# The state products of the sample tokens in one rounded pass over 128 rows, and the prompt's gated states on 128 rows

## The chip, the cores and the metric

The kernel runs on one core of one Trainium2 chip. The metric is the device time of one launch in microseconds (us); lower is better. The kernel before took 2338.71 us, the median of three runs (2337.27 to 2346.19).

The engines are called here as the profile calls them: PE is TensorE's matmul side and PEld its weight loads, DVE is VectorE, ACT ScalarE, POOL GpSimd, SP SyncE.

## The reference

Two layers of a decoder trunk run on 512 prompt tokens and on 8 sequences of 4 new tokens ("the sample", 32 tokens in all). Per layer: a feed-forward block, a token mixer, a second feed-forward block. The mixer has four gated heads (GLA: keys of 64, values of 128) and four retention heads (keys and values of 128). Both keep a state of keys by values:

```
S_new = decay * S + einsum('bhsk,bhsv->bhkv', k * exp(b_last - b), v)
o     = o_inter(q, S) + einsum('bhts,bhsv->bhtv', A, v)
```

The prompt starts from zero states and goes through them in chunks; each of the 8 sample sequences has its own given states (state_gla, state_ret), which are read for the outputs, updated with 4 tokens each, and returned.

## The kernel before, in words

**Numbers.** All is float32. The weight products, nearly all of the work, are done with operands split in two rounded parts of type fp32r, a high and a low one: three products (high by high, low by high, high by low) replace one float32 product. All are issued on L500. The weights come by DMA into `raw`, ACT copies the high part into `w_hi` (L937), POOL subtracts to get `w_lo` (L445), and PE works through units of 8 key tiles with them. The small products of the mixer are plain float32; the profile lists two records for each of these.

**Mixer stage.** After the input projection (29 tiles of output, with the gates' and scores' steps between them) the prompt runs through four chunks of 128 tokens, c = 0 to 3, and the sample is a fifth step, S. For each chunk there are four PE steps, kept in the order written in TAIL_STEPS (for DVE and ACT in TAIL_HALF_STEPS):

- turn c: 14 transposes of values and keys to token-major form in PSUM; ACT copies them to `v_tok` and `k_tok` (L1085, L1087), DVE multiplies the retention keys with their decay (L1411).
- scores c: retention scores (L711), which DVE masks, and the chunk's state deltas (L717 retention, L722 gated), which DVE adds to the decayed states (L1446, L1453). `s_gla` holds the two heads of a pair one above the other: head p has partitions p*64 to p*64+63.
- out c: for each gated head a 128-row product of scores and values (L740) and, from chunk 1 on, a 64-row product of queries and state (L742); for each retention head two 128-row products (L747, L749).
- back c: outputs, scaled to unit mean square by ACT and DVE (squares L1092, sum L1463, root L1098 and L1101, product L1473), are transposed back (L763) and gated by DVE (L1485).

**Sample.** turn S gives `v_tok_s` and `k_tok_s`, 32 tokens on 32 partitions. Out S runs one product of scores and values per head (L776) and one per head and sequence with that sequence's state (L784, queries of the other sequences being zero), 64 rows for a gated and 128 for a retention head. POOL prepares these masked queries (mask_queries, L453 to L462), after `o_ready` of chunk 2. ACT starts the loads of the given states as soon as the last input tile is read (L1181, L1184).

**The sample's state deltas.** For each of the 8 heads, in UPDATE_ORDER (retention first), DVE spreads the head's values over 8 blocks of 128 columns, zero where a token is not of that block's sequence (mask_values, L1500), and PE multiplies the keys with two halves of 512 columns (sample_delta, L808): contraction over 32 tokens, float32. DVE adds the result to the state (L1511, L1517), ACT stores it. Delta 0 stands behind out S and is followed by two filler products (L519, keep_clock_up); deltas 1 to 7 stand behind the first seven of the eight units of the output projection. PE is in order, so a delta's time there is added to the projection's.

**Start.** ACT makes `half_gain`, half of the gains of all norms, once at the start (L1134). DVE converts the masks (L1550) before it waits for the first norm.

Of the kernel before, what the change touches and what calls it, by code (L numbers as in the profile page):

```python
# [28 lines left out]
P = 128  # L29
# [32 lines left out]
def trunk_kernel(nc, x_prompt, x_sample, state_gla, state_ret, norm_g, w1_gu, w1_down, w2_gu, w2_down,  # L62
# [64 lines left out]
    S = NCH  # L127

# [21 lines left out]
    with ExitStack() as ctx:  # L150
# [9 lines left out]
        def overlay(*tensors):  # L160
# [19 lines left out]
        half_gain = sb("half_gain", [P, DEPTH * NN * KD])  # L180
        chunk_decay = sb("chunk_decay", [P, QT, NCH + NS])
        rms = sb("rms", [P, 2, HA])
# [8 lines left out]
        ret_state, gla_state, v_tok_s, k_tok_s = overlay(  # L191
            ("ret_state", [P, HR, NS, DV], F32), ("gla_state", [P, QT, NS, DV], F32),
            ("v_tok_s", [TS, HA, P], F32), ("k_tok_s", [TS, HR * P + QT * P], F32))
# [20 lines left out]
        v_tok, k_tok, a_ret, s_gla, s_ret, o_tok = overlay(  # L214
# [3 lines left out]
            ("s_gla", [P, 2, QT, DV], F32), ("s_ret", [P, 2, HR, DV], F32),  # L218
            ("o_tok", [P, HA, P], F32))
# [15 lines left out]
        def v_by_batch(i):  # L235

            return v_tok[0:TS, (i + 1) % 2].rearrange("p h v -> p (h v)")[:, 0:NS * DV].rearrange("p (b v) -> p b v", b=NS)
# [24 lines left out]
        def post_gain(l, q, k):  # L262

            table = vecs if q == 1 else half_gain
            return table[:, bass.ds(l * (NN * KD) + ((2 * q + 1) * KD + k), 1)]
# [10 lines left out]
        x_turned = sem("x_turned")  # L276
        w_a2_loaded, a_loaded = sem("w_a2_loaded"), sem("a_loaded")
# [33 lines left out]
        o_turned, o_gated = sig("o_turned", NSTEP), sig("o_gated", NSTEP)  # L311
        v_masked, s_delta, s_updated = sig("v_masked", HA), sig("s_delta", HA), sig("s_updated", HA)
# [65 lines left out]
        STATE_DMAS = (2 + QT + HR) * 16  # L378
# [56 lines left out]
        def _(pool):  # L435
# [11 lines left out]

            def mask_queries(l):
# [39 lines left out]
        def _(pe):  # L488
# [192 lines left out]
            def turn(l, c_):  # L681
# [6 lines left out]
                elif c_ == 1:  # L688
                    wait(pe, o_normed, l, 0)
                elif c_ == 2:  # L690
                    wait(pe, in_read, l, NIN - 1)
                    wait(pe, o_gated, l, 0)
                else:
                    wait(pe, o_normed, l, c_ - 2)
                    wait(pe, o_gated, l, c_ - 2)
                for h in range(HA):
                    pe.transpose(ps[0:n, b0 + h // 4, h % 4 * P:(h % 4 + 1) * P], v_t[:, h, t0:t0 + n], ident)  # L697
                for h in range(HR):
                    pe.transpose(ps[0:n, b0 + 2, h * P:(h + 1) * P], k_r[:, h, t0:t0 + n], ident)
                for q in range(QT):  # L700
                    mm = pe.transpose(ps[0:n, b0 + 3, q * P:(q + 1) * P], k_dec[:, q, t0:t0 + n], ident)
# [24 lines left out]
            def out(l, c_):  # L726
# [9 lines left out]
                for h in range(HG):  # L736
# [30 lines left out]
            def out_sample(l, part):  # L767
# [4 lines left out]
                for h in range(part * HA // 2, (part + 1) * HA // 2):  # L772
# [3 lines left out]
                    pe.matmul(o, a_gla_s[:, p, q, :] if h < HG else a_ret_s[:, h - HG, :], v_tok_s[:, h, :], start=True,  # L776
                              stop=False)
# [16 lines left out]
            def sample_delta(l, i):  # L794

                h = UPDATE_ORDER[i]
                wait(pe, v_masked, l, i)
                if i >= 2:
# [3 lines left out]
                if h < HG:  # L802
                    p = h % 2
                    keys, r0, r1 = k_tok_s[:, HR * P + h * DKG:HR * P + (h + 1) * DKG], p * DKG, (p + 1) * DKG
                else:
# [100 lines left out]
        def _(act):  # L906
# [168 lines left out]
            def act_step(l, kind, c_):  # L1075
                n, b0 = TS if c_ == S else CH, BANK0[c_]
                if kind == "turn":
# [5 lines left out]
                    vt, kt = (v_tok_s, k_tok_s) if c_ == S else (v_tok[:, c_ % 2], k_tok)  # L1083
                    for i in range(2):
                        act.activation(vt[0:n, 4 * i:4 * i + 4, :],  # L1085
                                       ps[0:n, b0 + i, :].rearrange("p (h v) -> p h v", v=DV), ACT.Copy)
                    act.activation(kt[0:n, HR * P:(HR + QT) * P], ps[0:n, b0 + 3, 0:QT * P], ACT.Copy)\  # L1087
                        .then_inc(v_tok_ready.sem, 1)
# [15 lines left out]
                if kind == "root" and c_ == NCH - 1:  # L1104

                    wait(act, state_ready, l, c_)
                    act.dma_start(gla_p[l, 0].rearrange("(q p) k v -> (p k) q v", p=2), s_gla[:, c_ % 2, :, :])\
                        .then_inc(states_stored, 16)
# [25 lines left out]
            act.activation(half_gain[:, :], vecs[:, 0:DEPTH * NN * KD], ACT.Copy, scale=0.5).then_inc(vec_ready, 1)  # L1134
# [74 lines left out]
        def _(dve):  # L1209
# [192 lines left out]
            def turn_keys(l, c_):  # L1402
# [4 lines left out]
                if c_ == S:  # L1407
                    wait(dve, v_tok_ready, l, c_)
                n, b0 = TS if c_ == S else CH, BANK0[c_]
                kt, decay = (k_tok_s, c("k_decay_s", TS)) if c_ == S else (k_tok, c("k_decay"))  # L1410
                o = dve.tensor_tensor(kt[0:n, 0:HR * P].rearrange("p (h k) -> p h k", h=HR),  # L1411
                                      ps[0:n, b0 + 2, :].rearrange("p (h k) -> p h k", h=HR),
                                      decay.rearrange("p (h k) -> p h k", k=1).broadcast_to([n, HR, P]), ALU.mult)
                o.then_inc(k_tok_ready.sem, 1)
# [18 lines left out]
            def update_states(l, c_):  # L1433
# [7 lines left out]
                for q in range(QT):  # L1441
                    delta = ps[:, b0 + 3, (QT + q) * DV:(QT + q + 1) * DV]
                    if c_ == 0:
                        dve.tensor_copy(s_gla[:, new, q, :], delta)
                    else:
                        dve.scalar_tensor_tensor(out=s_gla[:, new, q, :], in0=s_gla[:, old, q, :],  # L1446
                                                 scalar=chunk_decay[:, q, c_:c_ + 1], in1=delta, op0=ALU.mult, op1=ALU.add)
# [47 lines left out]
            def mask_values(l, i):  # L1495

                h = UPDATE_ORDER[i]
                if i >= 2:
                    wait(dve, s_delta, l, i - 2)
                dve.tensor_tensor(v_by_batch(i), v_tok_s[:, h:h + 1, :].broadcast_to([TS, NS, DV]),  # L1500
                                  c("batch_mask", TS).rearrange("p (b x) -> p b x", x=1).broadcast_to([TS, NS, DV]),
# [19 lines left out]
            def dve_step(l, kind, c_):  # L1521
                if kind == "turn":
                    turn_keys(l, c_)
                elif kind == "scores":
                    decay_scores(l, c_)
                elif kind == "state":
# [21 lines left out]
            add_x_squares(0, 0)  # L1548
            dve.wait_ge(masks_loaded, 16)
            dve.tensor_copy(msk[:, :], mask_rows[:, :])  # L1550
            for l in range(DEPTH):
# [153 lines left out]
```

## Time and profile before

| | |
|---|---|
| median of three runs | 2338.71 us |
| profiled execution, its time | 2346.03 us |
| profiled execution, its span | 2344.2 us |
| PE busy | 2285.5 us (97%) |
| DVE busy | 820.4 us (35%) |
| ACT busy | 799.7 us (34%) |
| POOL busy | 943.7 us (40%) |
| DMA | 197.58 MB, mean 84 GB/s |

The profile is one execution, and its time is 7.3 us above the median of the runs. "Busy" of PE counts overlapped, modelled ends of matmuls, so the distance between starts tells more than durations do. PEclk is the clock granted to TensorE: 1.00 is 2.4 GHz and 0.50 is 1.2 GHz. The idle time in brackets at a row is that of the engine just before it, with what ended it.

### The profile page before, as it was taken

To read this page: it belongs to the slowest core of one execution; us is meant where nothing else is said; L and a number is where in the kernel's file an instruction comes from. 1 tells how busy PE (TensorE), PEld (TensorE's weight loads), DVE (VectorE), ACT (ScalarE), POOL (GpSimd) and SP (SyncE) were. 2 spreads that over 40 slices of the span, in tenths; PEclk is the share of its full clock that TensorE was granted. 3 is DMA by queue.
4 is the path that set the end of the run, shared out by engine and by line. 5 is a ranking of instruction groups with operands and counts; after the bars stand their busy time and mean duration, and the time that the engine had idled before them with its cause. 6 is when DMAs were issued, how large, how long until landed. Compare 5 with 4: busy or idle time off the path is not lost.

```text
span 2344.2 us, 43364 instructions
## 1 busy us (share of the span) xinstructions
PE 2285.5 (97%) x17703; PEld 2219.5 (95%) x17703; DVE 820.4 (35%) x1115; ACT 799.7 (34%) x1380; POOL 943.7 (40%) x770
## 2 busy tenths in 40 slices
PE   8999999999989999999999999999999999999998
PEld 8999999999968899999999999999998779999998
DVE  4222200687334522220052222017864454222102
ACT  4333333442312433233343333334323234333333
POOL 3444444344113344444534444443541124444442
PEclk9999999999989999999999999999999999999999
DMA  5323223222303223322322332332223132323222
GB/s 171 86 84 89 74 86 96 78 82 64 99 26 100 79 83 89 89 71 87 109 76 82 89 89 70 92 109 55 82 73 81 52 99 81 88 82 89 74 88 75
DMA packets 382556, 197.58 MB, mean 84 GB/s; under 512 B 8836, under 2 KB 381368, under 8 KB 382328
## 3 DMA queue, kind: packets, MB, share of 16 engines
q1 hardware_dynamic: 353200, 180.64, 26.8%
q10 hardware_dynamic: 29256, 15.49, 2.4%
q8 instruction: 77, 1.26, 0.2%
q14 instruction: 23, 0.19, 0.0%
HBM read 186.80 MB, written 9.31 MB: 84 GB/s over the span
## 4 chain that ended last, share of the span: by engine, by line
PE 93%; DVE 4%; ACT 1%; issue 1%; ACTq 0%; DMA 0%; DVEq 0%
PE ps L500 84%; PE ps L784 2%; PE ps L808 1%; PE ps L658 1%; DVE x L1275 1%; DVE xs_lo L1213 1%; DVE y L1269 0%; DVE y_out L1269 0%; PE ps L740 0%; PE ps L742 0%; PE ps L633 0%; PE ps L697 0%; DVE q_lvl L1360 0%; PE ps L763 0%; PE ps L747 0%
## 5 line engine op out<-in xcount | busy, mean ns | idle before, releaser
L445 POOL TENSOR_TENSOR w_lo<-raw,w_hi 128x512 fp32r<-128x512 f32 (+1 forms) x728 | 915.7, 1263 | 1281.5 <-ACT w_hi L937 1281.4
L500 PE MATMUL ps<-xs_hi,w_hi 128*128 128x256 f32 (+1 forms) x3712 | 789.6, 290 | 16.5 <-DVE xs_lo L1213 13.1
L500 PE MATMUL ps<-xs_lo,w_hi 128*128 128x256 f32 (+1 forms) x3712 | 786.4, 289 | 0.0
L500 PE MATMUL ps<-xs_hi,w_lo 128*128 128x256 f32 (+1 forms) x3712 | 784.2, 288 | 0.0
L937 ACT ACTIVATE w_hi<-raw 128x512 fp32r<-128x512 f32 (+1 forms) x728 | 420.8, 586 | 964.5 <-PE ps L500 964.0
L500 PEld LDWEIGHTS ps<-xs_hi,w_hi 128*128 128x128 f32 x3712 | 598.5, 188 | 25.4 <-DVE xs_lo L1213 15.2
L500 PEld LDWEIGHTS ps<-xs_hi,w_lo 128*128 128x128 f32 x3712 | 600.6, 188 | 0.0
L500 PEld LDWEIGHTS ps<-xs_lo,w_hi 128*128 128x128 f32 x3712 | 599.9, 188 | 0.2
L1234 DVE TENSOR_TENSOR tmp<-ps,rstd_pre 128x544 f32<-128x544 f32 x88 | 63.8, 725 | 642.4 <-PE ps L500 627.4
L500 PE MATMUL ps<-h_lo,w_hi 128*128 128x256 f32 x1272 | 267.4, 289 | 0.0
L500 PE MATMUL ps<-h_hi,w_lo 128*128 128x256 f32 x1272 | 266.6, 288 | 0.0
L500 PE MATMUL ps<-h_hi,w_hi 128*128 128x256 f32 x1272 | 266.5, 288 | 0.0
L500 PEld LDWEIGHTS ps<-h_hi,w_lo 128*128 128x128 f32 x1272 | 205.1, 188 | 0.0
L500 PEld LDWEIGHTS ps<-h_lo,w_hi 128*128 128x128 f32 x1272 | 204.8, 188 | 0.0
L500 PEld LDWEIGHTS ps<-h_hi,w_hi 128*128 128x128 f32 x1272 | 204.5, 188 | 0.0
L1254 DVE TENSOR_TENSOR acc<-acc,sq 128x544 f32<-128x544 f32 x30 | 21.8, 726 | 357.7 <-ACT sq L1020 357.7
L1240 DVE TENSOR_TENSOR tmp<-tmp 128x544 f32<-128x544 f32 x88 | 96.2, 1093 | 11.8 <-ACT tmp L981 4.1
L983 ACT ACTIVATE h_hi<-tmp 128x544 f32 (+1 forms) x88 | 57.9, 658 | 112.6 <-DVE tmp L1240 112.6
L1243 DVE TENSOR_TENSOR h_lo<-tmp,h_hi 128x544 f32 x88 | 64.0, 727 | 83.8 <-ACT h_hi L983 83.8
L1020 ACT ACTIVATE sq<-ps 128x544 f32<-128x544 f32 (+2 forms) x54 | 31.0, 575 | 148.1 <-PE ps L500 148.1
L1236 DVE TENSOR_TENSOR tmp<-ps,rstd_pre 128x544 f32<-128x544 f32 x88 | 62.9, 715 | 0.0
L981 ACT ACTIVATE tmp<-tmp 128x544 f32<-128x544 f32 x88 | 58.1, 660 | 11.1 <-DVE tmp L1234 0.9
(181 smaller groups left out, 1761.3 us busy)
## 6 DMA issues: line engine op xcount, KB each, us to landing
raw<-in_w_gu_dram SPq DMA_DIRECT2D x176, 512.0 KB, 3.8
raw<-in_w_in_dram SPq DMA_DIRECT2D x56, 512.0 KB, 3.8
raw<-in_w_down_dram SPq DMA_DIRECT2D x64, 384.0 KB, 3.4
raw<-in_w_down_dram SPq DMA_DIRECT2D x64, 320.0 KB, 3.1
raw<-in_w_out_dram SPq DMA_DIRECT2D x16, 512.0 KB, 3.9
ret_state<-in_state_ret_dram ACTq DMA_DIRECT2D x8, 512.0 KB, 6.1
out_dram<-ret_state ACTq DMA_DIRECT2D x8, 512.0 KB, 3.2
x_tok<-in_x_prompt_dram SPq DMA_DIRECT2D x4, 512.0 KB, 6.3
```

What stands on the lines that cost most here:

```text
L445: pool.tensor_tensor(lo, raw[:, u, k0:k0 + n, :], hi.bitcast(F32), ALU.subtract)\
L500: mm = pe.matmul(bank_part(bank, a), w, v[:, kx, TOK[a]], start=(start and n == 0), stop=(stop and n == 2))
L658: mm = pe.matmul(ps[:, 4 + 2 * (n % 2) + c_ // 2, at:at + CH].rearrange("p (a t) -> p a t", a=2), k_lvl[:, hh, c_ * CH:(c_ + 1) * CH], q_l ...
L784: mm = pe.matmul(o, queries, state, start=False, stop=(b == NS - 1))
L937: act.activation(hi, raw[:, u, k0:k0 + n, :], ACT.Copy).then_inc(hi_split, 1)
L981: act.activation(tmp[:, 0, :], tmp[:, 0, :], ACT.Silu).then_inc(gate_silu.sem, 1)
L983: act.activation(h_hi[:, bass.ds(i * 2 + par, 1), :], tmp[:, 0:1, :], ACT.Copy).then_inc(hh_ready.sem, 1)
L1020: act.activation(sq[:, m % 2, cols], pair(m % 2)[:, cols], ACT.Square).then_inc(y_sq.sem, 1)
L1234: dve.tensor_tensor(tmp[:, 0, :], pair(2 * par), rstd_pre[:, :], ALU.mult)\
L1236: dve.tensor_tensor(tmp[:, 1, :], pair(2 * par + 1), rstd_pre[:, :], ALU.mult)\
L1240: dve.tensor_tensor(tmp[:, 0, :], tmp[:, 0, :], tmp[:, 1, :], ALU.mult).then_inc(h_prod.sem, 1)
L1243: dve.tensor_tensor(h_lo[:, tile, :], tmp[:, 0:1, :], h_hi[:, tile, :].bitcast(F32), ALU.subtract)\
```

## The change

The sample's state deltas get a rounded (fp32r) product over 128 rows. The 32 tokens are put four times on the partitions, so that rows 0 to 31, 32 to 63, 64 to 95 and 96 to 127 hold the same tokens. The values' high part stands on the first two quarters and their low part on the last two; the keys' high part stands on quarters 0 and 2 and their low part on 1 and 3. One product of such operands sums all four combinations of high and low. For that POOL writes the tokens four times before the transposes (spread_sample), turn S transposes all 128 columns, ACT rounds and DVE subtracts. Second, `s_gla` is laid out by head: each head has a plane of 128 partitions, of which the other head's 64 are zero, so that out c uses the full `q_dec` with 128 rows. Third, `half_gain` goes: the gains of the outer norms are halved in place.

The diff, cut to its core:

```diff
@@ pool
+            def spread_sample(l):
+                wait(pool, in_read, l, NIN - 1)
+                for n, src, dst in ((HA, v_t, v_spread), (HR, k_r, k_spread[:, 0:HR, :]), (QT, k_dec, k_spread[:, HR:HR + QT, :])):
+                    o = pool.tensor_copy(dst.rearrange("p h (o t) -> p h o t", o=QUADS),
+                                         src[:, :, TP:T]....broadcast_to([P, n, QUADS, TS]))
+                o.then_inc(rows_spread.sem, 1)
...
+                        spread_sample(l)
                         mask_queries(l)
@@ pe, turn
+                if c_ == S:
+                    wait(pe, rows_spread, l, 0)
-                    pe.transpose(ps[0:n, b0 + h // 4, h % 4 * P:(h % 4 + 1) * P], v_t[:, h, t0:t0 + n], ident)
+                    pe.transpose(ps[:, b0 + h // 4, h % 4 * P:(h % 4 + 1) * P],
+                                 v_t[:, h, t0:t0 + n] if c_ < S else v_spread[:, h, :], ident)
...
@@ pe, out
-                        pe.matmul(o, q_dec[p * DKG:(p + 1) * DKG, q, t0:t0 + CH],
-                                  s_gla[p * DKG:(p + 1) * DKG, (c_ - 1) % 2, q, :], start=False, stop=True)
+                        pe.matmul(o, q_dec[:, q, t0:t0 + CH], s_gla[:, (c_ - 1) % 2, p, q, :], start=False, stop=True)
@@ pe, sample_delta
+                if i == 0:
+                    wait(pe, k_low, l, 0)
...
-                    keys, r0, r1 = k_tok_s[:, (h - HG) * P:(h - HG + 1) * P], 0, P
+                tile = HR + h // 2 if h < HG else h - HG
+                keys = k_split[:, tile * P:(tile + 1) * P]
                 for a in range(2):
-                    mm = pe.matmul(ps[r0:r1, 4 + 2 * (i % 2) + a, :], keys,
+                    mm = pe.matmul(ps[:, 4 + 2 * (i % 2) + a, :], keys,
                                    v_by_batch(i)[:, a * NS // 2:(a + 1) * NS // 2, :], start=True, stop=True)
@@ act, turn S
+                        for i in range(2):
+                            o = act.activation(v_split[:, 4 * i:4 * i + 4, :],
+                                               ps[:, b0 + i, :].rearrange("p (h v) -> p h v", v=DV), ACT.Copy)
+                    o.then_inc(v_tok_ready.sem, 1)
+                    if c_ == S:
+                        act.activation(k_split[:, KR:KR + KG], ps[:, b0 + 3, 0:KG], ACT.Copy)
+                        wait(act, k_decayed, l, 0)
+                        act.activation(k_split[:, 0:KR], tmp[:, 0, 0:KR], ACT.Copy).then_inc(k_high.sem, 1)
@@ act, store of the prompt's gated state: two DMAs of 64 partitions in place of one of 128
@@ act, start
-            act.activation(half_gain[:, :], vecs[:, 0:DEPTH * NN * KD], ACT.Copy, scale=0.5).then_inc(vec_ready, 1)
+            for l in range(DEPTH):
+                for n in (1, 5):
+                    g = vecs[:, (l * NN + n) * KD:(l * NN + n + 1) * KD]
+                    act.activation(g, g, ACT.Copy, scale=0.5).then_inc(vec_ready, 1)
@@ dve, turn_keys: the decay multiplies 128 rows into tmp, ahead of the wait for v_tok_ready; then
+                low = slice(P // 2, P)
+                dve.tensor_tensor(v_split[low, :, :], ps[low, b0:b0 + 2, :].rearrange("p a (h v) -> p (a h) v", v=DV),
+                                  v_split[low, :, :].bitcast(F32), ALU.subtract).then_inc(k_tok_ready.sem, 1)
+            def low_keys(l):
+                wait(dve, k_high, l, 0)
+                for at in (TS, 3 * TS):
+                    low = slice(at, at + TS)
+                    dve.tensor_tensor(k_split[low, 0:KR], tmp[low, 0, 0:KR], k_split[low, 0:KR].bitcast(F32), ALU.subtract)
+                    o = dve.tensor_tensor(k_split[low, KR:KR + KG], ps[low, BANK0[S] + 3, 0:KG],
+                                          k_split[low, KR:KR + KG].bitcast(F32), ALU.subtract)
+                o.then_inc(k_low.sem, 1)
@@ dve, update_states: for each pair q, one operation of 64 partitions per head p in place of one of 128
@@ dve, mask_values
-                dve.tensor_tensor(v_by_batch(i), v_tok_s[:, h:h + 1, :].broadcast_to([TS, NS, DV]),
+                dve.tensor_tensor(v_by_batch(i), v_split[:, h:h + 1, :].bitcast(F32).broadcast_to([P, NS, DV]),
@@ dve, start, behind add_x_squares(0, 0)
+            dve.memset(s_gla.rearrange("p n h q v -> p (n h q v)"), 0.0).then_inc(s_zeroed, 1)
+            dve.wait_ge(s_zeroed, 1)
...
+            dve.wait_ge(tables_loaded, 16)
+            for i in range(1, QUADS):
+                for name in ("k_decay_s", "batch_mask"):
+                    o = dve.tensor_copy(cst[i * TS:(i + 1) * TS, cc[name][0]:cc[name][1]], c(name, TS))
```

low_keys runs on DVE right behind decay_scores of S. `v_by_batch` now uses all 128 partitions of the two buffers that lie over `v_tok`, and is of type fp32r. The first two ACT copies of turn S (32 rows, for out S) stay.

## Rows read from the trace of the kernel before

**Rows 1.** The page: busy time of each engine, and the chain that ended last.
```profile
PE 2285.5 (97%) x17703; PEld 2219.5 (95%) x17703; DVE 820.4 (35%) x1115; ACT 799.7 (34%) x1380; POOL 943.7 (40%) x770
...
PE ps L500 84%; PE ps L784 2%; PE ps L808 1%; PE ps L658 1%; DVE x L1275 1%; DVE xs_lo L1213 1%; DVE y L1269 0%; DVE y_out L1269 0%; PE ps L740 0%; PE ps L742 0%; PE ps L633 0%; PE ps L697 0%; DVE q_lvl L1360 0%; PE ps L763 0%; PE ps L747 0%
```

**Rows 2.** Windows, out S, layers 0, 1: stretch, length; PE, PEld, DVE, ACT, POOL; PEclk.
```profile
668.07:694.59 26.52, 26.52 (x153) 19.67 (x153) 4.92 (x6) 0.80 (x3) 0.00 (x0) 0.68 0.06 15
1826.78:1845.32 18.54, 18.54 (x153) 15.08 (x153) 4.92 (x6) 0.80 (x3) 0.00 (x0) 1.00 0.08 23
```

**Rows 3.** Timeline of PE, output projection, layer 0: start, duration, instructions.
```profile
708.92 0.41 PE L500 MATMUL ps<-o_hi,w_lo 128*128 128x256 f32 x2
709.27 1.98 PE L808 MATMUL ps<-v_tok,k_tok_s 32*128 32x512 f32 x4
711.18 0.52 PE L500 MATMUL ps<-o_hi,w_hi 128*128 128x256 f32 x2
711.53 0.41 PE L500 MATMUL ps<-o_lo,w_hi 128*128 128x256 f32 x2
711.78 0.41 PE L500 MATMUL ps<-o_hi,w_lo 128*128 128x256 f32 x2
...
733.63 1.93 PE L808 MATMUL ps<-v_tok,k_tok_s 32*64 32x512 f32 x4
```

**Rows 4.** Timeline of PE, layer 1: out 2, scores 3, back 2.
```profile
1806.83 0.39 PE L740 MATMUL ps<-v_tok,a_gla 128*128 128x128 f32 x2
...
1810.39 0.39 PE L749 MATMUL ps<-s_ret,q_r 128*128 128x128 f32 x2
...
1811.95 1.06 PE L711 MATMUL ps<-q_r,k_r 128*128 128x128 f32 x8
...
1816.49 1.07 PE L763 MATMUL ps<-cst,o_tok 128*128 128x128 f32 x8 [1.37 <-issue]
```

**Rows 5.** Timelines of ACT and PE behind out 1, layers 0 and 1.
```profile
636.77 1.09 ACT L1092 ACTIVATE sq<-ps 128x512 f32<-128x512 f32 x2 [6.93 <-issue]
...
639.85 2.04 PE L711 MATMUL ps<-q_r,k_r 128*128 128x128 f32 x8 [2.73 <-DVE k_tok L1411]
...
644.00 1.09 PE L763 MATMUL ps<-cst,o_tok 128*128 128x128 f32 x8
...
1793.23 3.73 ACTq L1184 DMA_DIRECT2D gla_state<-in_state_gla_dram  x2
...
1800.16 1.13 PE L711 MATMUL ps<-q_r,k_r 128*128 128x128 f32 x8 [1.59 <-DVE k_tok L1411]
...
1802.71 1.09 PE L763 MATMUL ps<-cst,o_tok 128*128 128x128 f32 x8
```

**Rows 6.** Timelines of PE and ACT, layer 0: turn S to the start of out S.
```profile
660.43 1.03 PE L697 MATMUL ps<-cst,v_t 128*32 128x128 f32 x8 [1.15 <-DVE v_t L1485]
...
662.16 1.06 ACT L1085 ACTIVATE v_tok_s<-ps 32x512 f32<-32x512 f32 x2 [5.80 <-PE ps L701]
...
667.17 0.44 PE L711 MATMUL ps<-q_r,k_r 128*32 128x32 f32 x8
668.07 0.37 PE L776 MATMUL ps<-v_tok_s,a_gla_s 32*32 32x128 f32 x2 [0.46 <-DVE a_ret_s L1421]
```

**Rows 7.** Timeline of PE, layer 1: delta 0 and back S, behind out S.
```profile
1845.32 1.98 PE L808 MATMUL ps<-v_tok,k_tok_s 32*128 32x512 f32 x4
...
1849.76 0.65 PE L763 MATMUL ps<-cst,o_tok 32*128 32x32 f32 x8 [1.40 <-DVE o_tok L1473]
```

**Rows 8.** Timelines of POOL and DVE, output projection; last row: DVE at the start.
```profile
719.32 3.58 POOL L445 TENSOR_TENSOR w_lo<-raw,w_hi 128x512 fp32r<-128x512 f32 x2 [4.54 <-ACT w_hi L937]
...
735.60 2.15 DVE L1511 SCALAR_TENSOR_TENSOR gla_state<-gla_state,chunk_decay,ps 64x128 f32<-64x128 f32 x8 [0.48 <-PE ps L808]
737.67 1.51 DVE L1500 TENSOR_TENSOR v_tok<-v_tok_s,cst 32x1024 f32<-32x1024 f32 x1
...
40.40 0.72 DVE L1234 TENSOR_TENSOR tmp<-ps,rstd_pre 128x544 f32<-128x544 f32 x1 [4.03 <-ACT rstd_pre L921]
```

More of the change, by code:

```diff
@@ L127, in trunk_kernel @@
     S = NCH
+    QUADS = P // TS
+    KR, KG = HR * P, QT * P
     IN_ORDER = (1, 2, 3, 0) + tuple(range(4, NIN))
@@ L212, in trunk_kernel @@
             ("w_a2_sb", [2 * GR, QT * P], F32))
-        v_tok, k_tok, a_ret, s_gla, s_ret, o_tok = overlay(
+        v_tok, k_tok, a_ret, s_ret, o_tok, rms, v_ret_s = overlay(
             ("v_tok", [P, 2, HA, P], F32),
@@ L217, in trunk_kernel @@
             ("a_ret", [P, HR, CH], F32),
[L218 to L219 removed]
+            ("s_ret", [P, 2, HR, DV], F32),
+            ("o_tok", [P, HA, P], F32), ("rms", [P, 2, HA], F32), ("v_ret_s", [TS, HR, P], F32))
+        v_rows, = overlay(("v_rows", [P, 2, HA, P], F32R))
         _, y_out, o_lo, o_hi = overlay(("ahead_of_v_t", [P, 7 * QT * T + QT * HALF], F32), ("y_out", [P, KD, T], F32),
@@ L262, in post_gain @@
         def post_gain(l, q, k):
-            table = vecs if q == 1 else half_gain
-            return table[:, bass.ds(l * (NN * KD) + ((2 * q + 1) * KD + k), 1)]
+            return vecs[:, bass.ds(l * (NN * KD) + ((2 * q + 1) * KD + k), 1)]
+        tables_spread = sem("tables_spread")
         tables_loaded, masks_loaded, x_loaded = sem("tables_loaded"), sem("masks_loaded"), [sem(f"x_loaded{i}") for i in range(X_PARTS)]
@@ L311, in trunk_kernel @@
         o_turned, o_gated = sig("o_turned", NSTEP), sig("o_gated", NSTEP)
+        rows_spread = sig("rows_spread", 1)
+        k_decayed, k_high, k_low = sig("k_decayed", 1), sig("k_high", 1), sig("k_low", 1)
         v_masked, s_delta, s_updated = sig("v_masked", HA), sig("s_delta", HA), sig("s_updated", HA)
@@ L775, in out_sample @@
                     o = ps[0:TS, BANK0[S] + 2 * a, i * DV:(i + 1) * DV]
-                    pe.matmul(o, a_gla_s[:, p, q, :] if h < HG else a_ret_s[:, h - HG, :], v_tok_s[:, h, :], start=True,
-                              stop=False)
+                    pe.matmul(o, a_gla_s[:, p, q, :] if h < HG else a_ret_s[:, h - HG, :],
+                              v_gla_s[:, h, :] if h < HG else v_ret_s[:, h - HG, :], start=True, stop=False)
                     for b in range(NS):
@@ L1082, in act_step @@
                         wait(act, o_ready, l, c_ - 2)
-                    vt, kt = (v_tok_s, k_tok_s) if c_ == S else (v_tok[:, c_ % 2], k_tok)
                     for i in range(2):
[L1085 to L1088, printed above, removed]
+                        vt = (v_gla_s, v_ret_s)[i] if c_ == S else v_tok[:, c_ % 2, 4 * i:4 * i + 4, :]
+                        o = act.activation(vt[0:n, :, :],
+                                           ps[0:n, b0 + i, :].rearrange("p (h v) -> p h v", v=DV), ACT.Copy)
+                    if c_ < S:
+                        o = act.activation(k_tok[:, KR:KR + KG], ps[:, b0 + 3, 0:KG], ACT.Copy)
+                    else:
+                        for i in range(2):
[6 more added lines that the diff above has]
+                        act.activation(k_split[:, 0:KR], tmp[:, 0, 0:KR], ACT.Copy).then_inc(k_high.sem, 1)
                 elif kind == "squares":
@@ L1106, in act_step @@
                     wait(act, state_ready, l, c_)
-                    act.dma_start(gla_p[l, 0].rearrange("(q p) k v -> (p k) q v", p=2), s_gla[:, c_ % 2, :, :])\
-                        .then_inc(states_stored, 16)
+                    for p in range(2):
+                        act.dma_start(gla_p[l, 0].rearrange("(q p) k v -> p k q v", p=2)[p],
+                                      s_gla[p * DKG:(p + 1) * DKG, c_ % 2, p, :, :]).then_inc(states_stored, 16)
                     act.dma_start(ret_p[l, 0].rearrange("h k v -> k h v"), s_ret[:, c_ % 2, :, :])\
@@ L1406, in turn_keys @@
                     wait(dve, state_delta, l, c_ - 1)
[L1407 to L1414, printed above, removed]
+                b0 = BANK0[c_]
+                kt, decay = (tmp[:, 0, 0:KR], c("k_decay_s")) if c_ == S else (k_tok[:, 0:KR], c("k_decay"))
+                o = dve.tensor_tensor(kt.rearrange("p (h k) -> p h k", h=HR),
+                                      ps[:, b0 + 2, :].rearrange("p (h k) -> p h k", h=HR),
+                                      decay.rearrange("p (h k) -> p h k", k=1).broadcast_to([P, HR, P]), ALU.mult)
+                if c_ < S:
+                    o.then_inc(k_tok_ready.sem, 1)
+                    return
+                o.then_inc(k_decayed.sem, 1)
+                wait(dve, v_tok_ready, l, c_)
+                low = slice(P // 2, P)
[9 more added lines that the diff above has]
+                o.then_inc(k_low.sem, 1)
             def decay_scores(l, c_):
@@ L1442, in update_states @@
                     delta = ps[:, b0 + 3, (QT + q) * DV:(QT + q + 1) * DV]
[L1443 to L1447, printed above, removed]
+                    for p in range(2):
+                        rows = slice(p * DKG, (p + 1) * DKG)
+                        if c_ == 0:
+                            dve.tensor_copy(s_gla[rows, new, p, q, :], delta[rows])
+                        else:
+                            dve.scalar_tensor_tensor(out=s_gla[rows, new, p, q, :], in0=s_gla[rows, old, p, q, :],
+                                                     scalar=chunk_decay[rows, q, c_:c_ + 1], in1=delta[rows],
+                                                     op0=ALU.mult, op1=ALU.add)
                 for h in range(HR):
@@ L1525, in dve_step @@
                     decay_scores(l, c_)
+                    if c_ == S:
+                        low_keys(l)
                 elif kind == "state":
```

31 lines of the change are left out of this document (18 added, 13 removed).

## The prediction, made before the kernel after was run

> **What bounds the kernel now.** I read the page first, then the windows over out S, then PE's timeline stretch by stretch, and the other engines only where PE stood idle. On the page PE is busy for 97% of the span and the chain of waits lies on it; DVE, ACT and POOL are busy for 34 to 40% [rows 1]. So a microsecond taken from PE is a microsecond of the kernel wherever PE runs without a gap, and nothing where PE then waits for a chain that hasn't become shorter. The reader is to see two things in the rows. One is distances between starts: durations overlap. The other is the brackets: 2.73, 1.59, 1.37, 0.46 and 1.40 us are the gaps in the mixer's tail [rows 4 to 7].
>
> The profiled execution took 2346.03 us (span 2344.2 and 1.8 around it), 7.3 above the median of 2338.71. The windows show where: out S ran the same 153 matmuls in 26.52 us in layer 0 and 18.54 in layer 1, at a mean granted clock of 0.68 and of 1.00 [rows 2]. 2346.03 - 7.98 = 2338.05, the time of the two faster runs. So two of the three timed runs most likely lack this stretch at 1.2 GHz. I make the sum as a difference, check it against the profile, and take it from the median.
>
> **The state deltas, L808.** In the projection a delta takes from 709.27 to 711.18, 1.91 us in four records; a gated head's lasts 1.93 in place of 1.98, so 1.86 [rows 3]. It also slows its neighbours. A pair of L500 records (256 and 288 columns) goes in 0.25 us, 711.53 to 711.78; the pair ahead of the delta takes 0.35 to its start (708.92 to 709.27) and the pair behind it 0.35 (711.18 to 711.53) [rows 3]. I count these 0.2 as the cost of going from 128 rows to 32 and back, and they go. Together 2.11 and 2.06 us. In its place come two fp32r products of 512 columns over 128 rows. L500 is just such a product: 544 columns in 0.25, so 512 in 0.235 and two in 0.47 us. Gain 1.64 for a retention head and 1.59 for a gated one. Bounds: above, 1.91 if the products were free; below, 0.2 if they stayed as dear as the float32 ones and only the neighbours gained. I take 1.6, since L500's row is the same kind. Deltas 1 to 7 lie in the projection: 3 x 1.64 + 4 x 1.59 = 11.3 per layer, **22.6 us** for two.
>
> Delta 0 gives nothing. It stands behind out S, where PE waits 1.40 us for back S [rows 7]: ACT's squares, DVE's sum, the root and the norm product are all released by out S's end, not by the delta. 4.44 us after that end back S starts, before and after; the gap becomes about 2.9 us.
>
> What must keep up is the projection's period: (733.63 - 709.27) / 3 = 8.12 us now, about 6.5 then [rows 3]. POOL needs 3.58 in one (two rests), DVE 0.7 for the squares' sum, 2.15 for a gated state and 1.51 for a mask, 4.4 together [rows 8]. A mask on 128 rows in place of 32 has the same 1024 columns; I cost it the same, and at double it is 5.9, still below 6.5. Nothing new ends last.
>
> **Out c, L742.** Out 2 takes 1806.83 to 1811.95 = 5.12 us. The 18 records of its start, in which 128-row and 64-row products alternate, take 3.56 (0.198 each); the remaining 14, all on 128 rows, 1.56 (0.111 each) [rows 4]. On 128 rows throughout it is 32 x 0.111 = 3.57: 1.55 less. Bounds: 0 if the slow pace is not due to the alternation, 1.6 at most. I take 1.55, as the pace changes in one product, to one of equal columns.
>
> The Trainium skill speaks against this: "TensorE: Matmul & The Clock Gate", on LDWEIGHTS in "Step-by-step: what each phase is for", says that a load's time goes by its columns and the number of rows doesn't matter. By it, 128 rows for 64 would bring nothing, and the sum would lack the whole term. Here the columns are equal and the pace isn't, so the row decides, but whether rows or something else of these products sets it, no row shows; this is rival A.
>
> Where does 1.55 count? **Out 1: nothing.** Behind it PE waits for k_tok, DVE's product stands behind the sum of ACT's squares, and these start only when ACT has issued the loads of the states: 636.77 in layer 0 after 6.93 us of "issue", and in layer 1 the last issue ends at 1793.23 + 3.73 = 1796.96, just when out 1 ends [rows 5]. These issues are released by the last input tile, which doesn't move. The gaps grow from 2.73 to 4.3 us and from 1.59 to 3.1. **Out 2: in full.** Back 2 starts 4.54 us after out 2's end, by the squares' chain, with PE idle 1.37 before it [rows 4]; the chain moves along, and turn S behind it. **Out 3: in full, if turn S's copies keep up.** The 14 transposes of turn S have 128 columns on the moving side as before [rows 6]. ACT starts its copies at 662.16, two in 1.06 [rows 6]; now four of these, 2.12, until 664.3; then DVE's subtraction of 1024 columns, bounded by 1.06 (ACT's pace for as many columns) and the 1.51 of the mask [rows 8], say 1.35, near the mask, until 665.7. PE, with out 3 shorter, is at scores S at 667.17 - 1.55 = 665.6 [rows 6]. So about 0.1 us is lost, between -0.2 and +0.3 by the bounds. Four times 1.55 less twice 0.1: **6.0 us**.
>
> **Edits at nothing, and their cover.** The four subtractions of low_keys (at most half a mask each, 4 x 0.75 on DVE) delay the sum of squares 3; back 3 has the first half of out S, over 8 us of its 18.5 [rows 2], to hide the chain; without cover 3.0 a layer. The same cover hides k_low for delta 0. POOL's copies: 2304 columns, at the 1.79 us per 512 of its slowest subtraction [rows 8] 8 us, between the last input tile (about 628) and turn S at 660.43 [rows 6], and ahead of mask_queries, whose release by out 2 comes at 652; POOL's next splits wait for that anyway. The two more DVE operations per state update (2.15 / 8 = 0.27 each [rows 8]) stand behind the gates' products and no PE step waits for them at once. One more DMA issue on ACT, 0.4, falls into out S, where ACT is busy for 0.80 us [rows 2]; its landing is awaited long after. At the start the fill, six small copies and the wait for the tables (at most 1.5 + 6 x 0.3 = 3.3) fit DVE's 4.03 us wait [rows 8]; the four small halvings replace one on ACT, which then waits for x. Without cover these are 1 us once.
>
> **Sum.** 22.6 + 6.0 = 28.6. The profile's own time would be 2346.03 - 28.6 = 2317.4 with its slow stretch, the median 2338.71 - 28.6 = 2310.1. One thing I add: in layer 0 the clock fell at the 2.73 us gap (half clock, scores 2 took 639.85 to 644.00 = 4.15) and in layer 1 at 1.59 it did not (1800.16 to 1802.71 = 2.55) [rows 5]. Both gaps become longer than the one at which it fell, so I price one more fall, 1.6 us. **2311.7 us.**
>
> **Rivals.**
> A. Rows don't matter, only the deltas gain: 2338.7 - 22.6 + 1.6 = 2317.7. For: the page's rule above. Against: the pace changes within out 2.
> B. The stretch at 1.2 GHz in out S comes in the median run: + 8.0 = 2319.7, or in one place more behind out S. For: it came in the profile and, by its time, in the 2346.19 run; the gaps grow. Against: it was absent in layer 1 and, by the times, in two runs of three.
> C. The clock keeps up better, or the extra products cost less, or out 1 gives a part: 2310.1 minus layer 0's own 1.6 and up to 3.1 for out 1 = 2305.4.
> D. Slower. PE falls to 1.2 GHz at the longer gap behind out 1 and stays there until the projection, in both layers. Price per layer: out S 8.0 [rows 2], and out 2, scores 3, out 3 and the two turns, about 3.6 + 2.5 + 3.6 + 3.1 = 12.8 us more, so 20.8, or 41.6 in all: 2310.1 + 41.6 = 2351.7. It decides from the point where a gap of 3 to 4 us isn't made good by the dense work behind it. Against: in layer 0 it was, at 2.73, after one short fall.
> E. It doesn't do what it says: the new products cost like float32 ones, two records each at the pace of L808. Then only the neighbours' 0.2 x 14 = 2.8 and out c's 6.0 come: 2338.7 - 8.8 = 2329.9. Against: L500's fp32r products show one short record each.
>
> **Chances.** Forecast (2308 to 2315) 0.55; A 0.08; B 0.17; C 0.12; D 0.03; E 0.03; 0.02 for anything else that is slower. The range reaches from C to just past B: 2304 to 2321. Within 0.5% (11.7 us, about what can be told from no change) means above 2327.0: from E, and a part of B in both layers (2327.7), 0.05. Slower 0.03, faster 0.92.
>
> **What would show it.** Right: L808 with 32 records instead of 64, about 0.23 us apart on 128 rows; a projection's period of 6.5 us; L742 at 0.11 us with 128 rows; out 2 and 3 at 3.6 us; gaps of 3 to 4.3 behind out 1; back S still 4.4 us after out S's end; scores S without a gap of more than 0.5. Wrong: DVE or POOL named as releaser of a delta or of an L500 in the projection; a low PEclk in out S in both layers; out 2 still at 5.1.

## The result, and the profile after

The kernel after takes 2320.86 us, the median of six runs (2319.05 to 2326.82), against 2341.45 for the kernel before (six runs, 2337.19 to 2346.19). The ratio is 0.9913, 95% interval 0.9894 to 0.9933: 20 us less, 16 to 25 by the interval. Forecast were 27 less, to 2311.7, most likely 2308 to 2315. The time lies above that and at the upper edge of the wider range (2304 to 2321). The sum of the work was right almost to a tenth: the experiments below give 28.5 us for the forecast 28.6. About 8 us of it were given back, nearly all by TensorE's clock, where the forecast had put 1.6.

The page of the profiled execution (2320.91 us, span 2319.0), the lines that answer to [rows 1]:

```profile
PE 2251.9 (97%) x17671; PEld 2213.2 (95%) x17671; DVE 838.7 (36%) x1148; ACT 802.0 (35%) x1389; POOL 951.7 (41%) x776
...
PE ps L518 85%; PE ps L806 2%; PE ps L676 1%; DVE x L1309 1%; DVE xs_lo L1247 1%; DVE y_out L1303 0%; DVE y L1303 0%; ACTq L1218 0%; PE ps L785 0%; PE ps L651 0%; PE ps L717 0%; PE ps L734 0%; DVE q_lvl L1394 0%; PE ps L740 0%; PE ps L829 0%
```

L829 is the new state delta (32 records for 64), L518 the split products that were L500. ACTq L1218 is ACT's queue issuing the loads of the gated states. Before, the chain went through these issues (L1184) in layer 0 only, and in layer 1 through out 1 itself; now it goes through them in both layers. The timeline of PE in the projection, layer 0, as in [rows 3]:

```profile
699.78 0.41 PE L518 MATMUL ps<-o_hi,w_lo 128*128 128x256 f32 x2
700.03 0.63 PE L829 MATMUL ps<-v_rows,k_split 128*128 128x512 f32 x2
700.50 0.41 PE L518 MATMUL ps<-o_hi,w_hi 128*128 128x256 f32 x2
700.75 0.41 PE L518 MATMUL ps<-o_lo,w_hi 128*128 128x256 f32 x2
...
706.53 0.63 PE L829 MATMUL ps<-v_rows,k_split 128*128 128x512 f32 x2
```

A delta takes 700.03 to 700.50, 0.47 us for 1.91, and its neighbours keep their pace: 0.25 ahead and 0.25 behind, for 0.35 each. The period is 6.50 for 8.12. Out 2 and back 2 of layer 1, as in [rows 4]:

```profile
1789.48 0.39 PE L763 MATMUL ps<-v_tok,a_gla 128*128 128x128 f32 x2
...
1791.49 0.39 PE L771 MATMUL ps<-s_ret,q_r 128*128 128x128 f32 x2
...
1793.06 1.06 PE L734 MATMUL ps<-q_r,k_r 128*128 128x128 f32 x8
...
1797.60 1.07 PE L785 MATMUL ps<-cst,o_tok 128*128 128x128 f32 x8 [1.37 <-issue]
```

Out 2 takes 3.58 us for 5.12, and back 2 starts 4.54 behind it, as before. Behind out 1 it is otherwise. Timelines of ACT and PE, as in [rows 5]:

```profile
636.79 1.08 ACT L1122 ACTIVATE sq<-ps 128x512 f32<-128x512 f32 x2 [7.03 <-issue]
...
639.87 2.05 PE L734 MATMUL ps<-q_r,k_r 128*128 128x128 f32 x8 [4.34 <-DVE k_tok L1443]
...
644.61 1.48 PE L785 MATMUL ps<-cst,o_tok 128*128 128x128 f32 x8
...
1772.86 5.29 ACTq L1218 DMA_DIRECT2D gla_state<-in_state_gla_dram  x2
...
1781.28 1.31 PE L734 MATMUL ps<-q_r,k_r 128*128 128x128 f32 x8 [4.53 <-DVE k_tok L1443]
...
1785.28 1.18 PE L785 MATMUL ps<-cst,o_tok 128*128 128x128 f32 x8
```

ACT's squares start at the same moment (636.79 for 636.77), so PE's gap grows by what out 1 gained. In layer 1 the issues also lasted longer, to 1778.15, 9.1 us after the first one, for 7.6 before; there the gap is 4.5 for 1.6. Of these 2.9 us, 1.5 are what out 1 gained and 1.4 the longer issues. Turn S and back S, as in [rows 6, 7]:

```profile
659.83 1.06 PE L717 MATMUL ps<-cst,v_spread 128*128 128x128 f32 x8 [1.11 <-issue]
...
663.64 1.23 DVE L1452 TENSOR_TENSOR v_split<-ps,v_split 64x1024 fp32r<-64x1024 f32 x1 [1.07 <-ACT v_split L1112]
...
665.05 0.44 PE L734 MATMUL ps<-q_r,k_r 128*32 128x32 f32 x8
665.96 0.37 PE L798 MATMUL ps<-v_gla_s,a_gla_s 32*32 32x128 f32 x2 [0.46 <-DVE a_ret_s L1470]
...
684.50 0.74 PE L829 MATMUL ps<-v_rows,k_split 128*128 128x512 f32 x2
...
688.94 0.65 PE L785 MATMUL ps<-cst,o_tok 32*128 32x32 f32 x8 [2.84 <-DVE o_tok L1525]
```

Turn S costs nothing on PE: DVE's subtraction ends at 664.87, and out 3 keeps PE busy until scores S starts at 665.05. Back S starts 4.44 us after out S's end, and the gap ahead of it is 2.84. Last, windows over the stretches at 1.2 GHz within the mixer and the projection, PE alone (stretch, length, busy, PEclk, DMA share, GB/s):

```profile
638.60:645.40 6.80, 5.53 (x28) 0.50 0.28 67
689.80:696.60 6.80, 4.89 (x22) 0.50 0.01 2
1782.10:1785.50 3.40, 3.40 (x20) 0.50 0.02 5
1809.40:1826.50 17.10, 17.10 (x77) 0.50 0.09 23
1836.70:1843.50 6.80, 4.12 (x22) 0.50 0.01 2
```

They sum to 40.9 us; before they were 3.4, 17.1, 3.4 and 6.8, together 30.7. The 17.1 us in out S are called the long stretch from here on. In the kernel after each of the others begins in a gap of PE of 2.8 to 4.5 us or just behind it; the long stretch begins 3.1 us behind a gap of 0.46. The table has the distances between starts, in us, layers 0 and 1; the two columns with fillers are experiments told below, in which the clock stays up:

| from, to | before | before with fillers (before_fill) | after | after with fillers (fill_all) |
|---|---|---|---|---|
| out 1, out 2 | 17.8, 15.1 | 16.1, 15.1 | 18.9, 18.0 | 16.4, 15.0 |
| out 2, out 3 | 13.8, 13.8 | 13.8, 13.8 | 12.3, 12.3 | 12.3, 12.3 |
| out 3, first state product of out S | 6.4, 6.4 | 6.5, 6.5 | 4.9, 4.9 | 5.0, 5.0 |
| from there to delta 0 | 26.2, 18.2 | 18.2, 18.2 | 18.2, 26.2 | 18.2, 18.2 |
| delta 0, projection | 7.2, 7.2 | 7.2, 7.2 | 7.2, 7.6 | 7.2, 7.2 |
| projection, first to last product | 63.9, 65.3 | 62.6, 62.7 | 53.7, 52.8 | 51.5, 51.5 |

Both profiled executions happen to have one long stretch, so they differ by 25.1 us, more than the medians do.

### The profile page after: what moved, and what is told of

Read it like the earlier page. It is cut to its first block, busy times and chain, and to the rows that moved or that the text cites. A ratio compares the mean times of both kernels' runs of the same rounds, so it can differ in the third digit from the quotient of the medians.

```text
span 2319.0 us, 43349 instructions
## 1 busy us (share of the span) xinstructions
PE 2251.9 (97%) x17671; PEld 2213.2 (95%) x17671; DVE 838.7 (36%) x1148; ACT 802.0 (35%) x1389; POOL 951.7 (41%) x776
## 4 chain that ended last, share of the span: by engine, by line
PE 93%; DVE 4%; ACT 1%; issue 1%; ACTq 1%; DMA 0%; DVEq 0%
PE ps L518 85%; PE ps L806 2%; PE ps L676 1%; DVE x L1309 1%; DVE xs_lo L1247 1%; DVE y_out L1303 0%; DVE y L1303 0%; ACTq L1218 0%; PE ps L785 0%; PE ps L651 0%; PE ps L717 0%; PE ps L734 0%; DVE q_lvl L1394 0%; PE ps L740 0%; PE ps L829 0%
## 5 line engine op out<-in xcount | busy, mean ns | idle before, releaser
L518 PE MATMUL ps<-xs_hi,w_hi 128*128 128x256 f32 (+1 forms) x3712 | 787.4, 289 | 16.4 <-DVE xs_lo L1247 13.1
L518 PE MATMUL ps<-xs_hi,w_lo 128*128 128x256 f32 (+1 forms) x3712 | 785.5, 288 | 0.0
L518 PE MATMUL ps<-xs_lo,w_hi 128*128 128x256 f32 (+1 forms) x3712 | 782.7, 288 | 0.0
L518 PEld LDWEIGHTS ps<-xs_hi,w_hi 128*128 128x128 f32 x3712 | 604.0, 189 | 25.4 <-DVE xs_lo L1247 15.2
L518 PEld LDWEIGHTS ps<-xs_lo,w_hi 128*128 128x128 f32 x3712 | 603.5, 189 | 0.2
L518 PEld LDWEIGHTS ps<-xs_hi,w_lo 128*128 128x128 f32 x3712 | 600.1, 188 | 0.0
L518 PE MATMUL ps<-h_hi,w_lo 128*128 128x256 f32 x1272 | 267.2, 289 | 0.0
L518 PE MATMUL ps<-h_lo,w_hi 128*128 128x256 f32 x1272 | 266.1, 288 | 0.0
L518 PE MATMUL ps<-h_hi,w_hi 128*128 128x256 f32 x1272 | 265.6, 288 | 0.0
L518 PEld LDWEIGHTS ps<-h_hi,w_hi 128*128 128x128 f32 x1272 | 206.7, 189 | 0.0
L518 PEld LDWEIGHTS ps<-h_lo,w_hi 128*128 128x128 f32 x1272 | 206.1, 189 | 0.0
L518 PEld LDWEIGHTS ps<-h_hi,w_lo 128*128 128x128 f32 x1272 | 204.9, 188 | 0.0
```

The costliest lines, as they stand in the source:

```text
L518: mm = pe.matmul(bank_part(bank, a), w, v[:, kx, TOK[a]], start=(start and n == 0), stop=(stop and n == 2))
```

## The experiments

Two explanations stood for the missing 8 us. By the clock theory all of the work was saved, and PE then spent more time at 1.2 GHz; by the work theory less work was saved than summed. Every kernel was timed against the kernel before, in three groups. Each run gives a time and a mean granted clock. In the groups' 43 runs of the kernel before, 20 took 2337.4 to 2339.4 us at 0.995 or 0.996, and the other 23 took 2342.6 to 2353.8 at 0.989 to 0.994. That the 23 have the long stretch, and two of them (2353.6 and 2353.8) one in each layer, is inferred from time and mean clock; a trace shows it for the one profiled run. Medians of before in the groups (2339.2, 2344.7, 2339.4) therefore differ by which kind was more frequent; ratios carry that in their intervals, and where two of my kernels are compared I use their own times. The quickest runs of before agree between the groups (2337.4, 2337.6, 2337.5).

**The kernel after, again.** No edit.

> The kernel after, unchanged, timed again beside the others. Clock theory: the PE work saved is the full 28.6 us, and the rest was given back because TensorE's clock stands at 1.2 GHz for longer; then single runs scatter by steps of about 6 to 8 us around 2319 to 2327, and the ratio to before is 0.990 to 0.993. Work theory: less work was saved; then the runs scatter by under 2 us.

Measured: 2319.52 us (2319.10 to 2321.98), ratio 0.991 (0.9892 to 0.9928). Of 12 runs of this kernel, ten took 2319.1 to 2322.0 at a clock of 0.991 or 0.992, two 2326.6 and 2326.8 at 0.987. None took the 2312 that I estimate for a run without the long stretch (2319.5 - 8.0). At 0.992 the kernel before takes 2343.7 to 2346.8 and this one 2319.1 to 2319.7: 24 to 28 less at equal clock. This timing alone decides little, since its six runs lie within 2.9 us and show no step; the step of 7 us is in the first six. By their times all 12 have the long stretch that fewer than 6 in 10 had before; both profiled ones show it, one in layer 1 and one in layer 0.

**Only the state products.**

```diff
-                        pe.matmul(o, q_dec[:, q, t0:t0 + CH], s_gla[:, (c_ - 1) % 2, p, q, :], start=False, stop=True)
+                        pe.matmul(o, q_dec[p * DKG:(p + 1) * DKG, q, t0:t0 + CH],
+                                  s_gla[p * DKG:(p + 1) * DKG, (c_ - 1) % 2, 0, q, :], start=False, stop=True)
```

and update_states and the store as before.

> Only the sample's state products are changed; the prompt's gated states stay 64 rows high as before. Clock theory: the 22.6 us of the projection come in full, the gap behind out 1 stays at 1.6 to 2.7 us, and the time is 2341.5 - 22.6 = 2319, as good as the kernel after. Work theory (each part gives its share of what is missing): 22.6 x 0.72 = 16 less, 2325.

Measured: 2324.33 us (2318.06 to 2331.51), ratio 0.9935 (0.9911 to 0.9959). The median is the work theory's, 5 us above what the clock theory gave; the single runs go by their clock: 2318.06 at 0.995, 2323.5 to 2324.6 at 0.992 or 0.993, 2331.3 and 2331.5 at 0.990 and 0.989. Those at 0.992 to 0.993 are 19 to 23 below before at 0.992. The period in the projection is 6.50 in both layers, so the work came in full, and the long stretch came with it (layer 0 of its profile). The gap behind out 1 is 2.78 in layer 0 and 3.03 in layer 1, where before had 1.59, and the clock fell there for 3.4 us. Out 1 is no shorter in this kernel, so that gap grew by the issues alone: ACT's squares start 6.8 us after out 1's start, for 5.3 before. Over the ten profiles with all six issues in one go, layer 1 has one or the other: 5.2 to 5.3 in six, 6.7 to 6.8 in four, both profiles of the kernel after among these. Whether the change makes the longer one likelier is open.

**Only the gated states.** From the kernel before, with the layout of `s_gla`, the fill at the start and the halved gains.

> Only the prompt's gated states are laid out on 128 rows; the sample's state products stay float32 on 32 rows. Clock theory: out 2 and out 3 give 6.2 us, but the gap behind out 1 grows to 3 to 4.3 us, the clock falls there in both layers (about 2 us each and more behind it), and the time is within 3 us of before, 2336 to 2342. Work theory: 6.0 us less in full, 2335.

Measured: 2340.06 us (2332.55 to 2349.17, 12 runs), ratio 0.9996 (0.9974 to 1.0017): nothing to be told from no change. Out 2 to out 3 is 12.3 us and out 3 to out S 4.9, as in the kernel after, so 6.2 us are there. They show in part in the best runs, 2332.6 to 2335.2 at 0.993 to 0.995, against 2337.4 at 0.996; four of twelve runs took 2348.8 to 2349.2 at 0.988. This part alone makes the gap behind out 1 longer (4.46 and 3.06 us), the clock falls behind both, and the median has none of the 6.2 us.

**Fillers at all gaps.** To the kernel after:

```diff
                 if kind == "turn":
                     turn(l, c_)
+                    if c_ == 2:
+                        wait(pe, state_ready, l, 1)
+                        keep_clock_up(6, 5)
...
                 if c_ == S:
+                    wait(pe, state_ready, l, NCH - 1)
+                    keep_clock_up(1, 5)
                     out_sample(l, 0)
...
                     sample_delta(l, 0)
-                    keep_clock_up(WARM_NORM)
+                    keep_clock_up(WARM_NORM + 5)
...
                     step(l, kind, c_)
+                keep_clock_up(4)
                 out_projection(l)
```

The second argument is the PSUM bank.

> The kernel after with filler products of 256 columns in the gaps: 6 behind turn 2, 1 ahead of out S, 5 more behind delta 0, 4 behind back S. Clock theory: the clock stays at 2.4 GHz through the mixer, the gaps are no longer, and the time falls by 6 to 16 us below the kernel after, to 2305 to 2313. Work theory: no change from the kernel after, or slower by the fillers that do not fit (up to 3 us).

Measured: 2303.98 us (2303.49 to 2306.50), ratio 0.9846 (0.9826 to 0.9866), 0.997 to 1.0 mean clock. This beats the kernel after by 15.5 us (2319.52 in the same group; 16.9 from 2320.86) with more work on PE. Windows over 90 us of each layer, in its profile:

```profile
620.00:710.00 90.00, 83.33 (x661) 75.30 (x659) 51.41 (x86) 27.51 (x56) 17.48 (x17) 1.00 0.27 72
1760.00:1850.00 90.00, 84.72 (x670) 76.68 (x669) 52.95 (x84) 26.28 (x52) 21.03 (x19) 1.00 0.31 81
```

The clock is 1.00 throughout. PE behind turn 2 and behind delta 0, in the same profile:

```profile
635.33 2.76 PE L537 MATMUL ps<-cst 128*128 128x256 f32 x12
639.92 1.13 PE L734 MATMUL ps<-q_r,k_r 128*128 128x128 f32 x8 [1.83 <-DVE k_tok L1449]
...
682.67 3.18 PE L537 MATMUL ps<-cst 128*128 128x256 f32 x14
686.53 0.65 PE L787 MATMUL ps<-cst,o_tok 32*128 32x32 f32 x8 [0.68 <-DVE o_tok L1531]
```

Scores 2 starts at 639.92 for 639.87: the fillers stood in time that was lost anyway, and back 1 comes at full clock.

**One place at a time.** The same edits, only behind turn 2; only ahead of out S; only behind delta 0 and back S.

> The kernel after with 6 filler products behind turn 2 only, in the gap of 3 to 4.5 us. Theory that each gap costs on its own: the fall of the clock behind this gap (6.8 and 3.4 us at half) goes, 2 to 4 us less than the kernel after, 2316 to 2318, and out S still falls in some runs. Rival, that this gap is what brings the clock down in out S as well: most of the 15.5 us come, 2306 to 2309.

> The kernel after with one filler product ahead of out S only, where PE waits 0.46 us. Theory that out S falls by its own start (32-column products behind a wait): the stretch of 17.1 us no longer comes, 7 to 8 us less, 2311 to 2313. Rival, that it comes from the earlier gap: no change, 2319.

> The kernel after with 5 more filler products behind delta 0 and 4 behind back S. Theory that each gap costs on its own: the 6.8 us at half clock at the start of the projection goes in both layers, 6 to 7 us less, 2313. Rival, that these falls are fewer in other runs: 3 us or less.

Measured: fill_1 2315.13 us (2313.41 to 2316.14), ratio 0.9879 (0.9857 to 0.9902); fill_S 2313.42 (2311.95 to 2314.54), 0.9873 (0.9851 to 0.9896); fill_B 2311.11 (2306.71 to 2316.16), 0.986 (0.9835 to 0.9886). So each place costs something on its own: about 4.4, 6.1 and 8.4 us below the 2319.5 of after_again, which was timed in another group. They add up to 19 where all together give 15.5, so they are not quite independent. fill_1 takes the fall behind out 1 away and keeps the one in out S (1804.0, 17.1 us in its profile); it came out 0.9 below the expected range. With the filler ahead of out S the profile has no long stretch in either layer, and by their times none of the six runs has one; the median is 0.4 above the expected range. Windows over out S, layer 1, of the kernel after and of fill_S, as in [rows 2]:

```profile
1806.32:1832.83 26.51, 26.51 (x153) 19.54 (x153) 7.03 (x10) 0.80 (x3) 0.00 (x0) 0.68 0.06 15
```
```profile
1805.64:1824.18 18.54, 18.54 (x153) 15.08 (x152) 6.91 (x10) 0.68 (x3) 0.00 (x0) 1.00 0.09 22
```

One product of 256 columns a layer, in a wait of 0.46 us, is worth 8.0 us in this window and 6.1 in the median. Whether the filler's work does it, or only that PE's steps shift, is not separated: late, below, loses the stretch in five of six runs with no filler. For fill_B the rival (3 us or less) fell; three of its six runs, 2306.7 to 2308.1 at 0.997 or 0.998, must lack the long stretch as well, though nothing was put there. The median of fill_B lies between runs of both kinds, so its 8.4 is not the price of one place alone. Why a filler behind out S changes how often out S falls is open.

**The kernel before with fillers.** The same four places, 3, 1, 2 more and 4.

> The kernel before with fillers at the same four places, as many as its shorter gaps hold (3, 1, 2 more and 4). Clock theory: the clock stays up, the time falls below 2333, and the distance to the kernel after with fillers (2304.0) is the PE work alone, 28.6 us as summed, so 2332.6. Work theory: the distance is about 20, so 2324.

Measured: 2332.48 us (2331.85 to 2333.15, 10 runs), ratio 0.9951 (0.9936 to 0.9965), clock 0.998 to 1.0. The distance to fill_all is 2332.48 - 2303.98 = 28.5 us, where the sum said 28.6. The two kernels ran in two groups, whose runs of before at 0.996 were 2337.4 to 2338.0 and 2337.6 to 2338.0, so they compare directly. With the clock up, the work saved is what was summed, and the work theory is out. The clock cost the kernel before about 9 us (2341.45 - 2332.48) and the kernel after 17 (2320.86 - 2303.98); of the 17, 1.4 can be the longer issues of layer 1, which the profile of fill_all lacks.

**The loads issued later.** In ACT, without fillers and then with them (3 behind turn 2); `load_state` issues the loads whose numbers it is given:

```diff
-                for h in range(HR):
-                    act.dma_start(ret_state[:, h, :, :], ...).then_inc(states_loaded, 16)
-                for q in range(QT):
-                    act.dma_start(gla_state[:, q, :, :], ...).then_inc(states_loaded, 16)
+                load_state(l, (0, 1))
                 for kind, c_ in TAIL_HALF_STEPS:
                     act_step(l, kind, c_)
+                    load_state(l, {("root", 1): (2, 3), ("turn", 3): (4, 5)}.get((kind, c_), ()))
```

> The kernel after, without fillers; ACT issues only two of the six loads of the given states ahead of the mixer's tail, two behind the root of chunk 1 and two behind turn 3. If ACT's issue queue is what holds the squares of chunk 1 (and so scores 2), the gap behind turn 2 falls from 4.3 to about 1.5 us, 2.9 us per layer are gained there and the clock no longer falls there: 2319.5 - 5.8 - 2 to 4 = 2310 to 2312. Rival, that DVE's chain ends there anyway: gap and time stay within 1 us.

> The same late loads with fillers: 3 behind turn 2, 1 ahead of out S, 5 more behind delta 0, 4 behind back S. By the clock theory and the queue theory together 2304.0 - 5.8 = 2298.2. By the clock theory alone 2304.

Measured: late 2304.55 us (2303.82 to 2318.54), ratio 0.9853 (0.9829 to 0.9877); late_fill 2299.56 (2299.35 to 2299.64), ratio 0.9819 (0.9802 to 0.9837). ACT and PE of late, layer 0:

```profile
633.88 1.09 ACT L1133 ACTIVATE sq<-ps 128x512 f32<-128x512 f32 x2 [4.26 <-PE ps L771]
...
637.01 1.01 ACTq L1100 DMA_DIRECT2D ret_state<-in_state_ret_dram  x2
```
```profile
636.96 1.13 PE L734 MATMUL ps<-q_r,k_r 128*128 128x128 f32 x8 [1.57 <-DVE k_tok L1450]
```

The squares now wait for PE and not for "issue"; scores 2 starts 2.9 us earlier and the gap is 1.57. Out 1 to out 2 is 13.5 us in both layers, for 18.9 and 18.0. The six issues in pairs cost 1.0 us a pair; in one go they took 8.9 and 9.1. late came out 5.5 us below the lower end of what was expected. Its profile has no long stretch, and by the times only one run of six does (2318.54 at 0.989, 14 us above the others, so rather in both layers than in one); that a gap two chunks earlier matters for that is seen, not explained. late_fill is the best kernel of this study; it missed its 2298.2 by 1.4, of which 0.4 a layer is that three fillers end after k_tok is ready (scores 2 at 637.37 for 636.96). The other 0.6 are open.

## Why the prediction was right or wrong

**The state deltas: right.** 1.91 to 0.47 us in the projection, and 0.2 at the neighbours; the period fell by 1.62, forecast 1.64 and 1.59. Delta 0 gave nothing, back S at 4.44 us as said. POOL, DVE and ACT kept up: fill_all's projection is PE busy for all of its 51.5 us. Rival E (as dear as float32) is out, with 32 records 0.235 us apart.

**The gated states: right.** Out 2 went from 5.12 to 3.58 us, out 3 likewise; out 1 gave nothing, for the reason given, which late confirms by taking it away. Rival A, that rows don't matter, is out: L742's product of 64 rows became L765 of 128 rows with equal columns, and the pace went from 0.198 to 0.112. It isn't the 64 rows by themselves: in out S a row of 16 products of 64 rows, all of one height, runs at 0.116 each. Two timelines of the kernel before, PEld and PE of out 2 in layer 1, show what the alternation does:

```profile
1807.15 0.29 PEld L742 LDWEIGHTS ps<-s_gla,q_dec 64*128 64x128 f32 x2
...
1810.28 0.30 PEld L749 LDWEIGHTS ps<-s_ret,q_r 128*128 128x128 f32 x2
```
```profile
1807.15 0.49 PE L742 MATMUL ps<-s_gla,q_dec 64*128 64x128 f32 x2
```

Where the height stays at 128 rows, the load of a product starts 0.11 us ahead of it (1810.28, L749 itself at 1810.39 in [rows 4]); where it changes, load and product start together, so less of the load is hidden. The Trainium skill ("TensorE: Matmul & The Clock Gate", "Step-by-step: what each phase is for") says of the load alone that its rows don't matter. The trace agrees with that: one load lasts 0.18 to 0.19 us at 64 rows and 0.19 at 128. The prediction's "By it, 128 rows for 64 would bring nothing" took it for a rule on products in a stream, which it is not.

**Turn S and the edits at nothing: right, and better by 0.2.** The subtraction took 1.23, for 1.35 forecast, and it did not delay scores S. The spreading on POOL took 2.6 us (627.8 to 630.4), where 8 were estimated from the pace of its subtractions. Neither it nor low_keys is in the chain that ended last. Out 0 of layer 0 starts at 605.5 us in both profiles, so the start costs nothing either.

**The clock: the step that failed.** "Both gaps become longer than the one at which it fell, so I price one more fall, 1.6 us." The mechanism was named, and mis-sized by a factor of five: 17 us after against 9 before, 8 more. The table of distances, each kernel against itself with fillers, tells where it went in the two profiles:

- Behind out 1: 1.7 us before, 5.5 after, so 3.8 for the 1.6. The fall in layer 1 came as forecast; behind gaps of 3.06 and 2.95 us in gated_only and fill_B it came too. On top came the ACT issues, which I had taken as fixed (1.4), and a fall of 6.8 us for 3.4 in layer 0 (0.8). It is not the length of the gap that makes it 6.8: after_again fell for 3.4 us behind 4.47.
- In out S: 8.0 in either profile. But before, 20 of 43 runs are without the long stretch, and after none of 12, by their times. This is the larger part of the error, about 4 us between the medians and 8 against a run without it. I had taken 2338.71 as a run without it, which its time bears out, and then the median run of the kernel after as one of the same kind, which was not (rival B, chance 0.17).
- At the projection: 3.9 us in either. The falls there (3.4 and 6.8 us before, 6.8 and 6.8 after) were in the trace before, and I had seen the gap ahead of back S grow to 2.9 and charged nothing. It did no harm: the 3.9 are in both times.

The parts add up. The median of the 20 runs without the stretch is 2337.9, and 2337.9 - 28.6 + 3.8 + 8.0 = 2321.1, for 2320.86 measured. Why the clock falls 3 us into out S while PE is busy, and why after the change in every run, is open.

So the outcome is rival B in its mechanism, at 2320.9 for its 2319.7. That it is so close is partly luck: B has 2.2 us too little behind out 1 and starts 0.8 too high. Rival D, the clock staying down from out 1 to the projection, did not come: it rose again within 7 us behind each gap. Rival C's part, out 1's gain, did not come by itself; late got it by moving the loads.

## What to carry to other kernels

Where PE is the bound and runs in and out of waits, shortening its work lengthens the gaps ahead of the next wait, and each lengthened gap is to be priced by what the clock does behind it, not by the gap alone. The clock may also fall in a step whose own gap hasn't changed, as in out S here. Fillers in time that is lost anyway are the cheap test, here worth 15.5 us. Before an absolute forecast, the mean clock of each run tells whether the median is one kind of run or a mixture. A gain that ends in a gap is a pointer to the next thing to move: behind out 1 it was a queue of DMA issues on the engine that the chain needed.

## What the runs showed of the hardware

- The clock can be at 1.2 GHz for long with PE busy throughout. Out S is 153 records with no gap (after, layer 1), 32 or 64 rows by 32 columns in its first half, and eight transposes of 128 by 128 ahead of the second. The clock fell there at 1809.39, 3.1 us behind the start, and stayed down for 17.1 us; it rose at 1826.46, among the products of 128 rows by 32 columns of the second half. Seven of the twelve profiles have one such stretch, each of 17.1 us.
- float32 products whose height alternates between 128 and 64 rows, columns equal, run at 0.198 us each where 128 throughout gives 0.111; the load then starts with its product and not 0.11 us ahead. Around a product of 32 rows (L808), each of the two steps from and to 128 rows takes 0.35 us for 0.25.
- An fp32r product of 512 columns over 128 rows takes 0.235 us and a float32 one over 32 rows 0.95 in two records.
- Six loads of 512 KB issued by ACT in one go held its queue for 7.6 to 9.1 us; the same in pairs, with pauses between them, 1.0 us a pair.
